# Loading the activations of a down projection in three pieces instead of five, and later

## What is computed

```
def _swiglu(u, w_gate, w_up, w_down):
    return (jax.nn.silu(u @ w_gate) * (u @ w_up)) @ w_down

h = h + 0.5 * _swiglu(_rms_norm(h, ffn1_norm[l]), ...)     # D_MODEL 1024, D_FF 2816
h = mixer and cross-attention added to h
h = h + 0.5 * _swiglu(_rms_norm(h, ffn2_norm[l]), ...)
return _rms_norm(h, final_norm)
```

## Time and profile before

| | |
|---|---|
| median of 3 runs | 2116.82 us |
| lowest, highest | 2115.36, 2118.54 us |
| profiled execution: time, span | 2115.36 us, 2113.6 us |
| TensorE busy | 2044.9 us (97%) |
| VectorE, ScalarE, GpSimd busy | 67%, 30%, 58% |
| granted TensorE clock, mean | 0.986 |
| bytes moved by DMA | 286.38 MB, mean 135 GB/s |

### The profile page before, as it was taken

The page is one execution under the profiler, slowest core; times in us unless marked ns, Lnnn a source line. Parts: engine busy times, 40 slices in busy tenths (PEclk is TensorE's granted clock), DMA queues, the critical chain, the costliest instruction groups (busy, mean ns, idle before and its releaser), DMA issues.

```text
span 2113.6 us, 24489 instructions
## 1 busy us (share of the span) xinstructions
PE 2044.9 (97%) x9194; PEld 1677.3 (79%) x9194; DVE 1422.4 (67%) x1602; ACT 636.1 (30%) x979; POOL 1221.8 (58%) x802
## 2 busy tenths in 40 slices
PE   8899999999999999999999999899999999999997
PEld 4787778788888887888887888787788888888885
DVE  6667676575985979763324365547776776789688
ACT  5432222223444510001121122325322322234443
POOL 6378687788555443122333422136699999985551
PEclk9999999999999999999999999999999999999998
DMA  7422332337986454332113141211223223278763
GB/s 267 146 97 95 128 139 95 102 118 250 319 277 216 149 170 86 103 103 63 50 50 120 49 160 60 100 50 40 75 95 129 87 84 130 95 256 293 235 205 132
DMA packets 141077, 286.38 MB, mean 135 GB/s; under 512 B 12832, under 2 KB 38048, under 8 KB 140576
## 3 DMA queue, kind: packets, MB, share of 16 engines
q1 hardware_dynamic: 100816, 233.21, 32.6%
q10 hardware_dynamic: 40144, 51.61, 7.5%
HBM read 222.39 MB, written 63.42 MB: 135 GB/s over the span
## 4 chain that ended last, share of the span: by engine, by line
PE 77%; DVE 16%; POOL 2%; DMA 2%; issue 1%; ACT 1%; SPq 1%; DVEq 0%; ACTq 0%; POOLq 0%
PE ps L524 76%; DVE f_g L1790 2%; DMA d_act<-f_g 1%; DVE acc L1790 1%; DVE xt_lo L2343 1%; DVE sq L2156 1%; POOL start_room L1212 1%; DVE h L2362 1%; DVE ua_lo L1790 1%; DVE w_lo L2353 1%; DVE sq L2194 1%; DVE acc L2156 1%; DVE xb_lo L2087 1%; DVE acc L2196 1%; POOL w_lo L1116 1%
## 5 line engine op out<-in xcount | busy, mean ns | idle before, releaser
L1116 POOL TENSOR_TENSOR w_lo<-raw,w_hi 128x512 fp32r<-128x512 f32 x352 | 548.8, 1575 | 229.3 <-ACT w_hi L1351 229.0
L524 PE MATMUL ps<-xt_hi,w_hi 128*128 128x512 f32 x1320 | 516.0, 391 | 1.2 <-DVE xt_lo L2343 0.8
L524 PE MATMUL ps<-xt_hi,w_lo 128*128 128x512 f32 x1320 | 513.9, 389 | 0.0
L524 PE MATMUL ps<-xt_lo,w_hi 128*128 128x512 f32 x1320 | 513.9, 389 | 0.0
L1351 ACT ACTIVATE w_hi<-raw 128x512 fp32r<-128x512 f32 x462 | 277.5, 623 | 420.3 <-POOL raw L1144 263.1
L1124 POOL TENSOR_SCALAR w_hi<-raw 128x1024 fp32r<-128x1024 f32 x54 | 63.1, 1169 | 474.6 <-PE ps L524 474.6
L524 PEld LDWEIGHTS ps<-xt_hi,w_hi 128*128 128x128 f32 x1320 | 248.0, 188 | 56.4 <-issue 2.4
L524 PEld LDWEIGHTS ps<-xt_hi,w_lo 128*128 128x128 f32 x1320 | 247.9, 188 | 51.5
L524 PEld LDWEIGHTS ps<-xt_lo,w_hi 128*128 128x128 f32 x1320 | 248.1, 188 | 51.0
L1144 POOL TENSOR_TENSOR raw<-raw 128x512 f32<-128x512 f32 x178 | 273.7, 1547 | 13.8 <-DMA raw<-in_gu 6.5
L524 PE MATMUL ps<-ua_hi,w_hi 128*128 128x512 f32 x608 | 238.7, 393 | 7.4 <-DVE ua_lo L1790 4.6
(11 more groups left out here) (310 smaller groups left out, 2887.3 us busy)
## 6 DMA issues: line engine op xcount, KB each, us to landing
raw<-in_dn SPq DMA_DIRECT2D x264, 256.0 KB, 3.5
raw<-in_gu SPq DMA_DIRECT2D x88, 512.0 KB, 5.9
raw<-in_weights SPq DMA_DIRECT2D x54, 512.0 KB, 3.5
d_act<-acc SPq DMA_DIRECT2D x20, 512.0 KB, 2.8
d_act<-sq SPq DMA_DIRECT2D x20, 512.0 KB, 3.8
d_act<-f_g SPq DMA_DIRECT2D x20, 512.0 KB, 4.7
xt_hi<-d_act SPq DMA_DIRECT2D x20, 512.0 KB, 5.6
xt_lo<-d_act SPq DMA_DIRECT2D x20, 512.0 KB, 4.7
```

The costliest lines, as they stand in the source:

```text
L524: ins = nc.tensor.matmul(out, lhsT, rhs, start=start, stop=stop)
L1116: add(lo, src, hi.bitcast(F32), op=ALU.subtract).then_inc(s_w_low["pool"], 1)
```

## The change

`ACT_CHUNKS` has three pieces, of four, four and two tiles (1 MB, 1 MB, 512 KB), instead of five. With it the two places that issue the pieces change. `before_down` issues the pieces of a sub-product in three successive steps instead of at every second of ten, and starts at later steps: 16, 24, 34, 46 and 57 instead of 6, 16, 26, 40 and 51. The explicit wait for the end of the gate/up stage, ahead of the loads of sub-products 2 and 3, is taken out. `first_acts` issues six loads instead of ten, with the same tiles requested at the same places. The number of semaphores `s_acts` falls from 20 to 12.

```
-ACT_CHUNKS = ((0, 2), (2, 4), (4, 6), (6, 8), (8, 10))
+ACT_CHUNKS = ((0, 4), (4, 8), (8, 10))
@@ before_down
-                for s, first, emptied in ((2, 6, None), (3, 16, None), (4, 26, 0), (5, 40, 2), (6, 51, 3)):
-                    if d == first and emptied is None:
-                        sp.wait_ge(s_gstep, GU_N * (f + 1))
-                    elif d == first:
+                for s, first, emptied in ((2, 16, None), (3, 24, None), (4, 34, 0), (5, 46, 2), (6, 57, 3)):
+                    if d == first and emptied is not None:
                         sp.wait_ge(s_a_lo, DN_N * f + FP * (emptied + 1))
-                    if first <= d < first + 2 * len(ACT_CHUNKS) and (d - first) % 2 == 0:
-                        act_load(f, s, (d - first) // 2)
+                    if first <= d < first + len(ACT_CHUNKS):
+                        act_load(f, s, d - first)
@@ first_acts
-                for at, s, c in ((1, 0, 0), (1, 0, 1), (1, 0, 2), (1, 0, 3), (2, 0, 4), (2, 1, 0), (2, 1, 1),
-                                 (7, 1, 2), (7, 1, 3), (7, 1, 4)):
+                for at, s, c in ((1, 0, 0), (1, 0, 1), (2, 0, 2), (2, 1, 0), (7, 1, 1), (7, 1, 2)):
```

## The result

The changed kernel took 2134.97 us (median of 4 runs, 2132.18 to 2135.83), the kernel before in the same session 2117.68 us. The ratio is 1.008, 95% interval 1.0061 to 1.0097. The forecast was 2116.7 with no change; the time lies outside its range, on the side of the rival that had 5%. The profiled execution took 2131.39 us (span 2129.6), the shortest of the five, 16.0 us more than the profiled one of before.

What follows compares the result with a forecast made beforehand. TensorE was taken as the bound. Issue time, first chunk (0 to +2.4), moved loads and removed wait cost 0, TensorE's waits -0.1: 2115.3 us profiled, median 2116.7, range 2113.8 to 2120.2.

Steps and rivals of the forecast that it cites:

- the rival that had 5%: Five activation bursts an FFN starve the weight blocks; each microsecond of landing beyond 12.4 us costs one per burst; 2127; 5%.
- What bounds the kernel: TensorE, busy 2044.9 of 2113.6 us; at most 0.8 us of its waits can be won in the down stages.
- Step 1, fewer DMAs: Fewer load issues free 1.8 us of ScalarE and 4.3 us of SyncE per FFN; TensorE waits for neither queue: 0.
- Step 2, the first 1 MB: Second FFN's activation 0 arrives as 1 MB, copied by 1878.2, before VectorE is free at 1878.41: cost 0, 0.2 us spare.
- the 7.5 of the bound: Second FFN: two 1 MB loads served evenly, the first landing after 7.5 us, would make TensorE wait 2.4 us more.
- Step 3, the moved loads and the removed wait: SyncE's later activation loads keep 30.8 to 41.3 us of slack; dropping the wait at step 6 gains nothing: 0.
- Step 3, the denser queue: SyncE's queue around steps 16 to 18: weights behind 2.62 MB of activations land in 10.1 us at most: cost 0.
- The limit: Weights of step 16 may land up to 12.4 us after their request before TensorE waits.
- The price of the rival: Ten bursts in all; weights landing at 13.4 us would cost 10 us, giving 2127; 5%.
- Even service: The second FFN's first 1 MB loads are served evenly: +2.4 us, 2119.2; 6%.
- small gain: Relief reaches VectorE's chain and TensorE's waits in the down stages go: -0.8 us, 2116.0; 6%.
- What I said would show it: Weights near step 16 landing in 4 to 8 us; TensorE waits near 16-20, 24-28, 34-38, 46-50 or 57-61 would disprove it.

Runs made afterwards that it cites:

- big_spread: Changed kernel with SyncE's three large pieces four steps apart instead of one, from steps 16, 27, 37, 47, 58: 2121.17 us, ratio 1.0018.
- small_late_spread: Changed kernel with SyncE's activations in five small pieces two steps apart, from steps 16, 26, 36, 46, 57: 2118.95 us, ratio 1.001.
- act_queue: Changed kernel with the 15 loads an FFN of sub-products 2 to 6 issued from ScalarE's queue instead of SyncE's: 2122.94 us, ratio 1.0023.

## Why the prediction was wrong

- *What bounds the kernel.* Right: the loss is TensorE made idle in the two down stages.
- *Step 1, fewer DMAs.* Right for ScalarE's side, 0 (ratio 0.9998). For SyncE's no run takes the issue time alone.
- *Step 2, the first 1 MB.* Nearly: it was issued at 1883.15 and copied at 1888.77, so it needed some 5.6 us, between the 4.9 I took and the 7.5 of the bound. VectorE idled 0.67 us and the wait at step 3 grew from 0.54 to 0.92 us. In the run of that side alone the piece took as long and VectorE idled 0.61 us, but the wait at step 3 was 0.56 us and the time shows no loss.
- *Step 3, the moved loads and the removed wait.* Right as far as the activations' own arrival goes: later still costs nothing (`big_spread`, `small_late_spread`).
- *Step 3, the denser queue: "cost 0 at both ends".* This is the step that failed; the rival of 5% was the mechanism. The limit was nearly right: 12.4 us from request to landing. (By luck in part: its chain takes off ScalarE's copy of the weights twice and leaves out VectorE's low half of them, 0.97 us, which stands ahead of the activation's.) Two things ahead of it were wrong.
  - The landing. I let the load move at 396 GB/s and put 6.2 to 6.4 us, 10.1 at most. (For 1.7 MB ahead my own rule gives 3.5 + 4.3 = 7.8 us, not 6.4.) Measured at the first burst were 5.8 to 10.0 us a block, at the second up to 10.1, and 10.8 from a step's first request to its last landing. From 555 to 561, as the first burst began, the queues moved 247 and 295 GB/s, not 396. And the queue itself issued more slowly: the second 1 MB piece took 1.1 to 1.2 us instead of 0.43, a step's two weight blocks up to 1.4 us instead of 0.8.
  - The lead. I gave every burst the lead of the kernel before, 20.2 us from request to step. But a request waits for a buffer, the buffer for VectorE's low half, and that is late after a burst. The weights of step 26 were requested 17.5 us before their step (585.22; undisturbed start 602.7), with some 10 us for landing instead of 12.4, and landed after 10.8. Eight steps were too few to win the lead back: one burst alone costs nothing, the pair costs 5 us, and the whole row 17. (Only of the densest burst, all at once, does the first cost by itself.)
- *The price of the rival.* It was put at 10 us for ten bursts that each overstep the limit by 1 us. In fact not every burst costs, and a late one delays several steps; the measured 17 us is larger.
- *Even service, small gain.* Not seen: the first of the two 1 MB pieces landed 5.6 us after its issue, the second 8.1, and TensorE's waits grew.
- *What I said would show it.* The waits came at 25 to 29, 35 and 70: in or near the named places, except 70. The weight loads near step 16 landed in 5.8 to 10.0 us, not in 4 to 8.

Open: the down stages explain 11 to 12 us, the medians differ by 17. Part of the rest may be the clock between the stages, where the traces of the kernel before differ among themselves by 3.6 us. The changed kernel's profiled execution was the shortest of five (2131.39 against up to 2135.83); what the longer ones lost I have not seen. Nor is it settled why small pieces at the same steps cost a third; their weights landed 1.2 us sooner, and near the limit such a difference counts fully, but no run took the issue time apart from the size. No version beat the kernel before: its down stages have 1 to 2 us of idle time in all.

## What to carry to other kernels

When bulk loads and just-in-time loads share the DMA engines, a few large loads are not free because they are few: here either size or density alone cost 0.2%, both together 0.8%. Spread them so that the small load behind always lands within its lead, and count the lead at the second and third burst, not only in a quiet stretch. Look at who waits one or two engines upstream: here ScalarE changed from waiting for TensorE to waiting for weights before TensorE had its first gap. And follow the in-order programs to their end: a late weight block held back a ready activation of the step before, on two engines.

## What the hardware showed beyond this

- A small load is late behind a large one on the other queue as well. In `act_queue` the two weight blocks that SyncE issued at 559.15 and 559.52, 0.7 and 1.1 us after ScalarE's 1 MB piece (558.43), landed after 6.1 and 8.1 us. In the changed kernel the two issued 1.5 and 1.8 us after the piece on their own queue took 5.8 and 7.3 us. The Trainium skill (DMA: Bandwidth & Descriptors, section Issuing engines are not separate DMA queues) says that DMAs of several issuing engines run on the same DMA engines, and that issuing from several only saves issue time. At this first burst the trace agrees; at the second the weights landed 2 us sooner with the other queue (6.7 against 8.8 us), with the pieces further apart.
- The response is far from linear: +24, +17, +2 us for 0, 1, 2 steps of spacing.
